# Two more raw weight slots, 128-row bias products and a row-per-partition regrouping of the second expert matrix in a one-core decoder step

## The reference, cut to what matters

```
logits = h @ router_w + router_b
top_v, top_e = lax.top_k(logits, TOP_K)
gates = softmax(top_v)
...
a = xe @ w1[e] + b1[e]
glu = minimum(a[:, 0::2], 7.0)
lin = clip(a[:, 1::2], -7.0, 7.0)
act = glu * sigmoid(1.702 * glu) * (lin + 1.0)
y = act @ w2[e] + b2[e]
```

## Time and profile before

| what | value |
|---|---|
| median of 3 runs | 1720.49 us (1716.52 to 1726.71) |
| profiled execution, its own time | 1719.83 us |
| its span in the profile | 1718.0 us |
| PE busy, share of the span | 92% |
| PE weight load | 73% |
| DVE | 71% |
| ACT | 59% |
| DMA moved | 475.98 MB, mean 277 GB/s |
| granted TensorE clock, mean | 0.956 |

### The profile page before, as it was taken

How to read it: one execution, slowest core, us unless ns; L and a number is a source line. 1 busy time by engine, 2 the same in 40 slices (tenths; PEclk the granted TensorE clock), 3 DMA queues, 4 the chain that set the end, 5 groups by cost and what they waited for, 6 DMA issues and landing times.

```text
span 1718.0 us, 23429 instructions
## 1 busy us (share of the span) xinstructions
PE 1575.5 (92%) x7948; PEld 1261.0 (73%) x7949; DVE 1225.9 (71%) x1035; ACT 1006.0 (59%) x894; POOL 401.4 (23%) x403
## 2 busy tenths in 40 slices
PE   5899679995799999999999999999999999999960
PEld 5898345885678777777777777777777787887750
DVE  3322951127577888888888888888888888888858
ACT  4323543014466766677676766776767677676642
POOL 1000000002333223222322232224223322332211
PEclk9899689997899999999999999999999999999995
DMA  7233125322688999999999999999999998999946
GB/s 216 82 119 108 46 74 187 126 102 78 244 296 333 340 348 341 356 347 342 344 354 338 352 338 350 339 344 348 352 341 358 349 353 337 357 355 332 347 148 261
DMA packets 109856, 475.98 MB, mean 277 GB/s; under 512 B 14410, under 2 KB 27354, under 8 KB 76433
## 3 DMA queue, kind: packets, MB, share of 16 engines
q1 hardware_dynamic: 98073, 449.85, 71.4%
q0 software_dynamic: 11744, 25.61, 4.0%
HBM read 468.62 MB, written 23.74 MB: 287 GB/s over the span
## 4 chain that ended last, share of the span: by engine, by line
PE 73%; DVE 11%; DMA 7%; ACT 4%; issue 4%; POOL 1%; ACTq 0%; DVEq 0%; SPq 0%; POOLq 0%
PE ps L1604 51%; PE ps L1340 8%; DVE lo L930 4%; DMA raw<-w 4%; ACT hi L633 3%; PE ps L1583 3%; PE ps L1609 3%; PE ps L1501 2%; DVE arena L1304 2%; PE ps L1477 2%; DMA raw<-w_in 1%; PE ps L1462 1%; PE ps L1577 1%; DMA arena<-h_rows,idx_g 1%; DVE arena L1027 1%
## 5 line engine op out<-in xcount | busy, mean ns | idle before, releaser
L930 DVE TENSOR_TENSOR lo<-raw,hi 128x2048 fp32r<-128x2048 f32 x396 | 893.5, 2289 | 203.6 <-ACT hi L633 203.5
L633 ACT ACTIVATE hi<-raw 128x2048 fp32r<-128x2048 f32 x396 | 745.9, 1913 | 227.7 <-DMA raw<-w 161.5
L1604 PE MATMUL ps<-hi,t_hi 128*128 128x512 f32 x1536 | 457.7, 406 | 11.4 <-DVE t_lo L1207 6.5
L1604 PE MATMUL ps<-lo,t_hi 128*128 128x512 f32 x1536 | 435.6, 392 | 0.0
L1604 PE MATMUL ps<-hi,t_lo 128*128 128x512 f32 x1536 | 434.6, 391 | 0.0
L1604 PEld LDWEIGHTS ps<-hi,t_hi 128*128 128x128 f32 x1536 | 273.8, 189 | 100.0 <-DVE lo L930 34.0
L1604 PEld LDWEIGHTS ps<-lo,t_hi 128*128 128x128 f32 x1536 | 289.8, 189 | 64.1
L1604 PEld LDWEIGHTS ps<-hi,t_lo 128*128 128x128 f32 x1536 | 289.9, 189 | 62.4
L583 POOL DMA_INDIRECT expert_rows<-arena,idx_s x32 | 84.2, 2631 | 493.2 <-ACT arena L834 493.2
L814 ACT ACTIVATE t_hi<-ps 128x1024 fp32r<-128x1024 f32 x65 | 66.4, 1022 | 114.9 <-PE ps L1583 114.9
L1340 PE MATMUL ps<-hi,t_hi 128*128 128x256 f32 x400 | 117.6, 294 | 11.9 <-ACT raw L691 8.4
(11 more groups left out here) (220 smaller groups left out, 1216.2 us busy)
## 6 DMA issues: line engine op xcount, KB each, us to landing
raw<-w SPq DMA_DIRECT2D x384, 1024.0 KB, 6.8
raw<-w_in SPq DMA_DIRECT2D x8, 1024.0 KB, 5.4
raw<-cache_k SPq DMA_DIRECT2D x32, 256.0 KB, 3.4
raw<-cache_v SPq DMA_DIRECT2D x32, 256.0 KB, 3.3
raw<-w_out SPq DMA_DIRECT2D x4, 1024.0 KB, 5.0
arena<-expert_rows SPq DMA_DIRECT2D x2, 2048.0 KB, 13.4
hi<-expert_rows SPq DMA_DIRECT2D x2, 2048.0 KB, 22.1
raw<-x_prompt SPq DMA_DIRECT2D x4, 512.0 KB, 3.6
```

Of the source, the lines that this page charges most:

```text
L633: act_e.activation(hi[:, slot, :], raw[:, slot_raw, :], ACT.Copy).then_inc(s_hi, 1)
L930: v.tensor_tensor(lo[:, slot, :], raw[:, slot_raw, :], hi[:, slot, :].bitcast(F32), ALU.subtract).then_inc(s_lo, 1)
L1604: last = pe.matmul(ps[:, base_bank + b, :], lhs[l][:, row, :], r[:, ck.slot(j), at:at + 512], start=first_k and kk == 0 and q == 0, stop=F ...
```

## The change

It does six things, all in or for the expert loop.

1. Raw slots become six. Four keep their own memory, two lie in the arena, in the room of `glu` and `y_sb` and beyond. The loads of chunks 4 and 5 of the first expert now wait for the router's sums (`s_n2`, `s_rk`) and the first gather; from chunk 6 on a load waits for the sixth chunk before it.
2. `glu` is gone: ACT writes the gated half straight into `act`, and DVE multiplies in place. ACT's L828 now waits that the former activations have been transposed.
3. `y_sb` shares its memory with `lin`: ACT's copy L834 also waits that DVE has read `lin`, and DVE's first clamp waits that the former scatter has landed.
4. `bias_r` and both selectors get 128 rows; rows 64 to 127 are zero (a POOL memset at the start).
5. A partition receives rows 8p + 2k and 8p + 2k + 1 of w2 in chunk k, which are one run of 8 KB in DRAM.
6. So transposed block k of the activations must hold every eighth column, k, k + 8, ...: the weight load of these eight transposes reads with a step of eight floats. The transposes of gathered rows stay as they were.

```diff
-RAW, RING = 4, 4
+RAW, RAW_OWN, RING = 6, 4, 4
-A_ACT, A_G, A_SIG, A_L, A_Y, A_TMP = 7168, 8192, 9216, 10240, 11264, 12288
+A_ACT, A_L, A_RAW = 7168, 8192, 9216
-        bias_r = sb("bias_r", [2 * NE, 3 * D], F32R)
-        sel_w1 = sb("sel_w1", [2 * NE, P], F32R)
+        bias_r = sb("bias_r", [P, 3 * D], F32R)
+        sel_w1 = sb("sel_w1", [P, P], F32R)
...
+        y_sb = lin
+        def raw_at(s):
+            return raw[:, s, :] if s < RAW_OWN else A(A_RAW + CH * (s - RAW_OWN), CH)
...
-                    src = a["w2"][0][bass.ds(e, 1), 256 * k:256 * k + 256, :].rearrange("a (k p) n -> p (a k) n", p=P)
+                    src = a["w2"][0][bass.ds(e, 1), :, :].rearrange("a (p k) n -> p (a k) n", k=KT)[:, 2 * k:2 * k + 2, :]
...
+                if j == RAW_OWN:
+                    sp.wait_ge(s_n2, NT)
+                    sp.wait_ge(s_rk, 1)
...
+            pool.memset(bias_r[:].bitcast(F32), 0.0)
...
             def gated(m, half, w1_done):
                 if half == 0 and (not isinstance(m, int) or m > 0):
-                    act_e.wait_ge(s_ac, m * 2)
+                    act_e.wait_ge(s_at, m)
-                act_e.activation(glu[:, cols], src[:, 0, :], ACT.Gelu_apprx_sigmoid).then_inc(s_s, 1)
+                act_e.activation(act[:, cols], src[:, 0, :], ACT.Gelu_apprx_sigmoid).then_inc(s_s, 1)
-            def y_out(m, done):
+            def y_out(m, done, lin_read):
                 act_e.wait_ge(s_pc, done)
+                act_e.wait_ge(s_ac, lin_read)
...
-            def clamp(m, half, w1_done):
+            def clamp(m, half, w1_done, stored):
+                if stored is not None:
+                    v.wait_ge(s_sca, stored)
...
-                if not isinstance(m, int) or m > 0:
-                    v.wait_ge(s_at, m)
-                v.scalar_tensor_tensor(out=act[:, cols], in0=glu[:, cols], scalar=GATED_TOP, in1=lin[:, cols],
+                v.scalar_tensor_tensor(out=act[:, cols], in0=act[:, cols], scalar=GATED_TOP, in1=lin[:, cols],
...
             def act_transposes(m):
-                row_transposes(act, s_ac, m * 2 + 2, s_at)
+                row_transposes(act.rearrange("p (c k) -> p k c", k=KT), s_ac, m * 2 + 2, s_at)
```

More of the change, by code:

```diff
@@ L157, in sem @@
             return ctx.enter_context(nc.semaphore(name))
-        raw = sb("raw", [P, RAW, CH])
+        raw = sb("raw", [P, RAW_OWN, CH])
         hi = sb("hi", [P, RING, CH], F32R)
@@ L222, in build @@
         vals_c = t_hi[:, NT, 3 * P:3 * P + 2 * NT].rearrange("p (t b) -> p t b", b=2)
-        act, glu, lin, y_sb = (A(v, D) for v in (A_ACT, A_G, A_L, A_Y))
+        act, lin = A(A_ACT, D), A(A_L, D)
+        y_sb = lin
+        def raw_at(s):
+            return raw[:, s, :] if s < RAW_OWN else A(A_RAW + CH * (s - RAW_OWN), CH)
         g2, h2_t, rw = A(A_G2, D), A(A_H2T, 2, D), A(A_RW, KT, NE)
@@ L409, in load_expert @@
                 if second_half:
[L410 to L411 removed]
+                    src = a["w2"][0][bass.ds(e, 1), :, :].rearrange("a (p k) n -> p (a k) n", k=KT)[:, 2 * k:2 * k + 2, :]
+                    dst = raw_at(ck.raw_slot(j)).rearrange("p (k n) -> p k n", k=2)
                 else:
                     src = a["w1"][0][bass.ds(e, 1), P * k:P * k + P, :].rearrange("a p n -> (a p) n")
[L414 removed]
+                    dst = raw_at(ck.raw_slot(j))
                 return sp.dma_start(dst, src).then_inc(s_raw[ck.raw_slot(j)], 16)
@@ L632, in split_hi @@
                 act_e.wait_ge(s_raw[slot_raw], loaded)
-                act_e.activation(hi[:, slot, :], raw[:, slot_raw, :], ACT.Copy).then_inc(s_hi, 1)
+                act_e.activation(hi[:, slot, :], raw_at(slot_raw), ACT.Copy).then_inc(s_hi, 1)
             def pro_hi(g):
@@ L663, in biases @@
                 act_e.wait_ge(s_b1, 1)
-                act_e.activation(bias_r[:], ar[0:2 * NE, 0:3 * D], ACT.Copy).then_inc(s_bh, 1)
+                act_e.activation(bias_r[0:2 * NE], ar[0:2 * NE, 0:3 * D], ACT.Copy).then_inc(s_bh, 1)
             def lambda_exps():
@@ L816, in selector @@
             def selector(dst, e):
-                return act_e.activation(dst[:], cst[0:2 * NE, bass.ds(C_EYE + e, 1)].to_broadcast([2 * NE, P]), ACT.Copy)
+                return act_e.activation(dst[:], cst[:, bass.ds(C_EYE + e, 1)].to_broadcast([P, P]), ACT.Copy)
             def gated(m, half, w1_done):
@@ L858, in body @@
                     if j == 2:
-                        y_out(n - 1, ck.number(0) - PRO)
+                        y_out(n - 1, ck.number(0) - PRO, n * 2 + 2)
                 rows_hi(n, s_at, s_ah, act_hi)
@@ L875, in _ @@
                 expert_hi(tail, j)
-            y_out(NE - 2, tail.number(0) - PRO)
+            y_out(NE - 2, tail.number(0) - PRO, 2 * NE)
             rows_hi(NE - 1, s_at, s_ah, act_hi)
@@ L894, in further @@
                     expert_hi(ck, j)
-                y_out(i + NE, ck.number(PER) - PRO)
+                y_out(i + NE, ck.number(PER) - PRO, i * 2 + (2 * NE + 2))
                 act_e.wait_ge(s_sca, i * 16 + 16 * (NE + 1))
@@ L929, in split_lo @@
                 v.wait_ge(s_hi, hi_done)
-                v.tensor_tensor(lo[:, slot, :], raw[:, slot_raw, :], hi[:, slot, :].bitcast(F32), ALU.subtract).then_inc(s_lo, 1)
+                v.tensor_tensor(lo[:, slot, :], raw_at(slot_raw), hi[:, slot, :].bitcast(F32), ALU.subtract).then_inc(s_lo, 1)
             def pro_lo(g):
@@ L959, in _ @@
             v.wait_ge(s_bh, 1)
-            v.scalar_tensor_tensor(out=bias_r[:], in0=bias_r[:].bitcast(F32), scalar=cst[0:2 * NE, C_NEGM:C_NEGM + 1],
+            v.scalar_tensor_tensor(out=bias_r[0:2 * NE], in0=bias_r[0:2 * NE].bitcast(F32), scalar=cst[0:2 * NE, C_NEGM:C_NEGM + 1],
                                    in1=ar[0:2 * NE, 0:3 * D], op0=ALU.mult, op1=ALU.add).then_inc(s_bh, 1)
@@ L1222, in gate_lin, with gating @@
                 v.wait_ge(s_s, m * 2 + (half + 1))
-                if not isinstance(m, int) or m > 0:
-                    v.wait_ge(s_at, m)
-                v.scalar_tensor_tensor(out=act[:, cols], in0=glu[:, cols], scalar=GATED_TOP, in1=lin[:, cols],
+                v.scalar_tensor_tensor(out=act[:, cols], in0=act[:, cols], scalar=GATED_TOP, in1=lin[:, cols],
                                        op0=ALU.min, op1=ALU.mult).then_inc(s_ac, 1)
-            def gating(m, w1_done):
-                clamp(m, 1, w1_done)
-                clamp(m, 0, w1_done)
+            def gating(m, w1_done, stored=None):
+                clamp(m, 1, w1_done, stored)
+                clamp(m, 0, w1_done, None)
                 gate_lin(m, 0)
@@ L1267, in body @@
                     expert_lo(ck, j)
-                gating(n + 1, ck.number(W1C) - PRO)
+                gating(n + 1, ck.number(W1C) - PRO, None if isinstance(n, int) else n * 16)
                 expert_lo(ck, 11)
@@ L1287, in further @@
                     expert_lo(ck, j)
-                gating(i + NE, ck.number(W1C) - PRO)
+                gating(i + NE, ck.number(W1C) - PRO, i * 16 + 16 * NE)
                 rows_lo(i + NE, s_ah, s_al, act_lo, act_hi)
@@ L1578, in index_product, with row_transposes @@
                 last.then_inc(s_ix, 1)
-            def row_transposes(src, wait, value, done):
+            def row_transposes(tiles, wait, value, done):
                 pe.wait_ge(wait, value)
                 for k in range(KT):
-                    last = pe.transpose(ps[:, 6 + k // 4, P * (k % 4):P * (k % 4) + P], src[:, P * k:P * k + P], ident)
+                    last = pe.transpose(ps[:, 6 + k // 4, P * (k % 4):P * (k % 4) + P], tiles[:, k, :], ident)
                 last.then_inc(done, 1)
@@ L1588, in x_transposes @@
                     pe.wait_ge(s_xl, m)
-                row_transposes(xg, s_gat, gathered * 16, s_xt)
+                row_transposes(xg.rearrange("p (k c) -> p k c", c=P), s_gat, gathered * 16, s_xt)
             def act_transposes(m):
-                row_transposes(act, s_ac, m * 2 + 2, s_at)
+                row_transposes(act.rearrange("p (c k) -> p k c", k=KT), s_ac, m * 2 + 2, s_at)
             def expert_chunk(ck, j, lhs, k, banks, first_k, bias):
```

6 lines of the change are left out of this document (3 added, 3 removed).

## The result

The changed kernel takes 1681.9 us (median of 4 runs, 1677.85 to 1682.89) where the one before takes 1720.7 beside it: a ratio of 0.976, 95% interval 0.974 to 0.978. The forecast was 1708; the time is that of the rival "the step is free", 1684. The profiled execution took 1682.89 us, with a span of 1681.1 where the span before was 1718.0.

A forecast was written before the change was run, and what follows sets the result against it. PE was taken as first bound, with DVE, ACT and DMA close behind. 1719.8 - 27.0 (bias rows) - 9 (slots) + 23.8 (step of eight) = 1707.6, say 1708 us; range 1681 to 1722.

The forecast's parts named there:

- the step is free: Rival: activation transposes reading every eighth column cost PE nothing; passes of 36.7 us, 1684 us in all; chance 0.28.
- Term 3: Activation transposes of every eighth column: slower weight loads delay PE, 23.8 us more over 256 transposes.
- The term's lower end: Least price of the activation transposes' step of eight on PE: 0 us.
- Term 3's upper end: Activation transposes: 0.267 us per weight load in place of 0.11, 40 us more on 256 transposes.
- Term 1: Bias groups of w1 and w2 with 128 rows: PE's pause around the 64-row groups goes, 27.0 us less.
- Term 2: Six raw slots in the expert loop: late chunk landings no longer stop PE, 9 us less.
- The DMA engines followed: Claim that DMA can feed the expert loop: 13.6 MB in a 36.7 us pass, 371 GB/s, with little left.
- What was costed at nothing: POOL's start memset, the first clamp's wait for a scatter, ACT's new waits and the first expert's reordered loads: no time added.
- The rival of a fourfold step: The step makes each activation transpose's load cost four times as much: 84 us more, 1768 us; chance 0.07.
- that of a pause with another cause: The bias pause does not come from the 64 rows, so 128 rows save nothing: 1735 us; chance 0.05.
- The rival that the slots bring nothing: Six raw slots gain nothing because the DMA engines, 0.93 busy, are at their end: 1717 us; chance 0.10.
- The forecast's own range: Total time of 1700 to 1722 us, said to come from the ends of the terms; forecast's chance 0.50.

The follow-up runs named there:

- regrouping alone: The kernel before with only w2 laid out by eight neighbouring rows and activations transposed by every eighth column: 1715.2 us, ratio 0.998.
- all but the regrouping: The changed kernel with the old order of w2 and transposes of neighbouring columns: 1681.4 us, ratio 0.978.
- the probes: The changed kernel with transposes reading other column steps, one execution each: four and two 1687.6 us, three and six 1693.1, five and eight 1682.0.

## Why the prediction was wrong

- **Term 3, where it failed.** The step that failed is "Between them and the matmuls is no idle time, so a slower load delays PE", with the 23.8 us put on it: "I take 23.8, since DVE's row is the one with a step." Nearly the whole of the miss, 26 us, is this term; it measured 0 (regrouping alone 0.998, all but the regrouping 1681.4). A load with a step of eight is longer, 0.187 us for 0.139, yet PE isn't delayed: the loads lie over one another, and what PE pays is the distance of their starts, which did not change (0.127 us for 0.126), so that eight transposes take 0.79 us as with neighbours. The recorded length was no price anyway: the expert matmuls' loads, which read neighbours, have 0.189 us on the mean in the same trace. The term's lower end, nothing, was the truth; the reason given for that rival, that loads read at half the rate of a stream and may have room, fits a step of eight in both places, but steps of two to six do cost something, so room is not all. That the time goes by the columns alone holds for the starts with a step of eight, and not for those with two to six, nor for the recorded lengths. Why eight is free stays open.
- **Term 3's upper end** was read from a stretch at another clock. It is the mean of this group:

```profile
L1452 PEld LDWEIGHTS ps<-arena x80: 186/310/394, 177.7 to 238.4; 128*128 128x128 f32 x80
```

  From 177 to 200 us the granted clock was 0.50, the lower of its two levels, from 177 to 239 us 0.66 on the mean, and in the loop 1.00. It wasn't the slowest full load either: two others took 0.337 us, at a granted clock of 0.50 (416 to 417 us). In the probes no load of the transposes took more than 0.243 us (the run with steps of three and six).
- **The rule on memory lines.** By the Trainium skill, Advanced Engine Details and Errata, section Memory Cachelines, an access pattern with one hit per 16-byte line should cost. The stream with a step of four agrees (twice the time), and so does DVE's sum (0.377 us for 0.286). The load with a step of eight does not (0.79 us for eight, as neighbours), nor the one with a step of two, which has two elements in a line and still costs (0.87 us).
- **Term 1 held, with a condition that the prediction lacked.** 27.0 forecast, 28.6 measured between six slots with 64 rows and with 128. On the four slots of before the same edit brought 6.3. The prediction added terms 1 and 2 as if each stood by itself. Here a saving on PE was only kept where the chunks came sooner too.
- **Term 2 held.** 9 forecast, 9.3 us measured alone, passes of 37.54 to 37.60 as the undisturbed one of 37.57. Five slots would do.
- **The DMA engines followed**: 358 GB/s in the stretch, which is 358 x 36.69 = 13.1 MB a pass; the prediction had counted 13.6, and so 371 GB/s, where the rows of before give 347 x 37.89 = 13.1 as well. No wait for a chunk is left.
- **What was costed at nothing** was nothing: the memset took 2.66 us from 2.16 on, and ACT first asked at 15.56; no clamp waited for a scatter; the first scatter starts at 512.8 as at 512.9 before.
- The rival of a fourfold step and that of a pause with another cause are out: 0.79 us for eight transposes, and bias groups at 0.91. The rival that the slots bring nothing is out by the 9.3 us.
- **The forecast's own range**, 1700 to 1722, is said to come from the ends of the terms. These add up to 1683 (1719.8 - 27.0 - 9.9) and 1741 (1719.8 - 19 + 40).

## What to carry to other kernels

Take the price of an operand's layout from the same engine and the same side of it: a step of 32 made DVE's sum a third longer, a step of eight cost PE's weight load nothing and one of four a tenth, and a step of four doubled PE's stream. Look at the distance of starts, not at the length of overlapping instructions. Where two edits relieve two resources that run close together, price the one on the kernel that has the other: here the bias rows are worth 6 us with four slots and 29 with six.

## What the runs showed that was not expected

The price of a step in the transposed operand does not grow with the step: for eight transposes 0.79 us with neighbours, 0.87, 0.83, 0.88, 0.83 and 0.97 with steps of two to six, 0.79 with eight. No theory that was written down ahead gives this order, and the cause stays open. And larger transfers, worth nothing with six slots, brought 0.7% with four and 128 bias rows.
